# Routing stage of a mixture-of-experts trunk: one choice of experts for the last two tiles, rows of slots in a matmul pass of their own, weighing on GpSimd, five low weight parts made early

## Chip, cores and metric

One core of a Trainium2 chip runs one program. The metric is the device time of one execution in microseconds (us). TensorE (PE), VectorE (DVE), ScalarE (ACT), GpSimd (POOL) and SyncE (SP, which here issues DMAs) run their own instruction streams and meet only at semaphores.

## What is computed

A decoder layer for 2048 tokens of width 1024: token mixing (gMLP and stick-breaking attention), cross-attention to 256 memory tokens, then a mixture of experts and a last norm. The change lies between the cross-attention and the experts:

```python
g_logits = t @ w_group + b_group;  p_group = softmax(g_logits);  g_sel = argmax(g_logits)
e_logits = (t @ w_router + b_router).reshape(T, 4, 8)[:, g_sel]
top_v, top_i = top_k(e_logits, 2)
gates = p_group[g_sel] * softmax(top_v);  eid = g_sel * 8 + top_i
# tokens sorted by expert, each expert padded to blocks of 128 slots
y = (silu(xb @ w1[e]) * (xb @ w3[e])) @ w2[e]        # per block of 128 slots
out = rmsnorm(x + sum over the two choices of gate * y)
```

## The kernel before

The program is a chain of blocks; between two of them all engines meet at a barrier, so the last engine to finish one sets the start of the next. All work is in tiles of 128 tokens (16 tiles). Products in full precision are made as three products of high and low parts (`split_product`, L73): high is a rounded copy by ACT, low is DVE's difference of the raw value and the high one.

**Cross block** (`attend_memory`, the step function is written once for each engine, and `rounds` calls it with b from -2 to 16). Step b has the scores of tile b+1, the output product of tile b and, for tile b-1, the residual sum, its norm (`hm_sb`, the input of the experts) and the logits: PE turns `hm_sb` (`turn_hm`, L1637), ACT makes the high part (L1499), DVE the low one (`low_hm`, L1542), PE multiplies with the router's weights (L1720), ACT copies the 72 rows of parts out (L1514), PE adds the parts (L1732), DVE adds the bias (`add_bias`, L1576). In the last step (b = 16) only the logits of tile 15 are left. DVE also chooses the experts there (`Picks.choose`, 22 small dependent operations from L1781 to L1801): tiles 0 to 13 in the step of b = 15, tile 14 in the step of b = 16, ahead of the bias of tile 15.

**Route block** (`route`, L1902). DVE chooses tile 15, then the gates; PE counts the ranks (`rank_ps`, L2053 to L2059); DVE makes from them the slot of each of 32 pairs of a choice and a tile (to L1995). Then, in four chunks of 8 pairs with two buffers, DVE makes `equal` (L2003: which of 66 blocks), `in_slot` (L2005: which of 128 lanes) and `in_block[..., 0]` (L2008: `equal` times the token number), ACT `in_block[..., 1]` (L2045: `equal` times the gate), and PE sums 32 products `in_slot` x `in_block` of 132 columns (L2069) into `slot_ps`, which holds the row and the gate of every slot. DVE copies both out (L2011, L2012), makes the tables of the blocks' experts (L2015 to L2021); POOL gathers the 128 rows of the first block from DRAM (L1885, L1890). Beside this SP loads the first two sets of expert weights, and ACT makes the eight high parts of the first set (L1875).

**Expert block** (`run_experts`). DVE makes the eight low parts of the first set (`cut_w13`, L1879), PE transposes the gathered rows (`transpose_x(0)`, L2319), ACT and DVE cut them (L2235, L2283), and the first product into `exp_g_ps` can begin. From there PE runs through all blocks of slots; SP loads an expert's weights as soon as PE has left the buffer.

`keep_busy` (L80) is a row of products of the identity with itself, whose result nobody reads. It stands at the start of the route block (16), behind the ranks (20), and in the expert block before (20) and behind (20) the first transposes.

```python
def keep_busy(pe, out, ident, count):
    for _ in range(count):
        pe.matmul(out, ident, ident, start=True, stop=True)
```

## Time and profile before

| | |
|---|---|
| median of 3 runs | 2640.78 us (2640.08 to 2641.35) |
| the profiled execution: own time, span | 2640.34 us, 2638.6 us |
| mean granted clock of TensorE | 0.981 |
| PE busy, PE weight load, DVE, ACT, POOL (share of the span) | 95%, 78%, 57%, 49%, 23% |
| cross block ends, route block starts | 1687.9 us, 1689.3 us |
| route block ends, expert block starts | 1720.8 us, 1721.3 us |
| first product of the experts | 1732.8 us |

Times in the trace are from the start of the span. A row of the timeline has its start, its duration, the engine and line, the tile written and those read, the shape, how many instructions are merged, and in brackets how long the engine was idle before it and who released it. A full-precision product on the identity or on the slots is two rows each ("x40" for 20 products); a transpose is one.

### The profile page before, as it was taken

What the parts mean: (1) busy time and instruction counts of PE and PEld (TensorE: products, weight loads), DVE (VectorE), ACT (ScalarE), POOL (GpSimd) and SP (SyncE); (2) the same over time, 40 slices, a digit from 0 to 9 for tenths busy, and PEclk for the clock granted to TensorE, in tenths of its full rate; (3) what the DMA queues carried; (4) which work ended last, traced back from release to release, by engine and by line L of the source; (5) the groups of instructions that cost most, each with busy time, mean ns of one, the idle gap of its engine ahead of it and who ended that gap; (6) DMA issues with size and microseconds to landing.
All of it is one profiled execution on the core that took longest, in us unless ns stands there. A gap on an engine that the chain in (4) does not pass through costs nothing. (4 is left out here: it accounts for less than half of the span.)

```text
span 2638.6 us, 44762 instructions
## 1 busy us (share of the span) xinstructions
PE 2507.8 (95%) x14474; PEld 2046.1 (78%) x14475; DVE 1497.0 (57%) x1976; ACT 1291.7 (49%) x2303; POOL 604.5 (23%) x653
## 2 busy tenths in 40 slices
PE   9999999999999999999999999799999999999991
PEld 7888888676666678886888888678877888888880
DVE  5221343698888864444333433666988755565653
ACT  5221211698899941133223322346878654465643
POOL 0000011477777720000000000012212212112223
PEclk9999999999999999999999999899999999999996
DMA  7433231314201033233121221448999865586757
GB/s 268 166 122 123 84 149 43 101 34 149 73 18 45 2 120 114 98 152 106 64 88 72 90 75 67 188 139 302 391 372 375 294 205 205 196 292 209 262 163 274
DMA packets 141439, 414.83 MB, mean 157 GB/s; under 512 B 22016, under 2 KB 30720, under 8 KB 140288
## 3 DMA queue, kind: packets, MB, share of 16 engines
q1 hardware_dynamic: 125040, 371.15, 38.1%
q0 software_dynamic: 13968, 33.59, 5.4%
q10 hardware_dynamic: 2304, 8.39, 0.8%
q8 instruction: 81, 1.33, 0.2%
q14 instruction: 46, 0.38, 0.0%
HBM read 338.60 MB, written 91.75 MB: 163 GB/s over the span
## 5 line engine op out<-in xcount | busy, mean ns | idle before, releaser
L685 POOL TENSOR_TENSOR stick_weight<-stick_weight,stick_left 128x512 f32<-128x512 f32 (+3 forms) x320 | 327.8, 1038 | 126.6 <-DVE stick_left L817 122.0
L1879 DVE TENSOR_TENSOR moe_w_lo<-moe_w_lo_raw,moe_w_hi (+1 forms) x256 | 298.9, 1220 | 62.7 <-ACT moe_w_hi L1875 34.7
L1875 ACT CAST moe_w_hi<-moe_w_lo_raw (+1 forms) x256 | 256.4, 1052 | 49.7 <-DMA moe_w_lo_raw<-in_w 32.0
L817 DVE TENSOR_TENSOR_SCAN stick_left<-stick_z_ps,stick_left,stick_any_row 128x512 f32<-128x512 f32 x192 | 240.2, 1275 | 35.2 <-ACT stick_z_ps L780 34.9
L778 ACT ACTIVATE stick_weight<-stick_z_ps 128x512 f32<-128x512 f32 (+3 forms) x320 | 173.7, 543 | 32.7 <-PE stick_z_ps L727 21.2
L740 PE MATMUL stick_t_ps<-all_ident,stick_weight 128*128 128x128 f32 x1088 | 165.0, 281 | 19.0 <-DVE stick_weight_t L825 9.2
L780 ACT ACTIVATE stick_z_ps<-stick_z_ps 128x512 f32<-128x512 f32 (+3 forms) x320 | 165.7, 518 | 10.2
L740 PEld LDWEIGHTS stick_t_ps<-all_ident,stick_weight 128*128 128x128 f32 x1088 | 115.6, 141 | 70.0 <-issue 45.4
L75 PE MATMUL exp_g_ps<-moe_w_hi,exp_x_hi 128*128 x376 | 151.2, 402 | 10.8 <-DVE exp_x_lo L2283 10.8
L1890 POOL DMA_INDIRECT moe_xg<-hm_scratch,moe_now x50 | 66.6, 1331 | 403.4 <-PE exp_x_ps L2319 296.3
L75 PE MATMUL proj_z_ps<-proj_w_hi,proj_h_hi 128*128 128x512 f32 x384 | 152.1, 396 | 2.5 <-DVE proj_h_lo L403 2.5
L2307 DVE TENSOR_TENSOR moe_w_lo<-moe_w_lo_raw,moe_w_hi 128x1024 f32 (+1 forms) x128 | 148.2, 1218 | 8.6 <-ACT moe_w_hi L2269 8.2
L75 PE MATMUL exp_y_ps<-moe_w_hi,exp_h_hi 128*128 128x512 f32 x376 | 150.4, 400 | 2.3 <-DVE exp_h_lo L2303 2.3
L76 PE MATMUL proj_z_ps<-proj_w_lo,proj_h_hi 128*128 128x512 f32 x384 | 150.2, 391 | 0.0
L77 PE MATMUL proj_z_ps<-proj_w_hi,proj_h_lo 128*128 128x512 f32 x384 | 150.0, 391 | 0.0
L77 PE MATMUL exp_y_ps<-moe_w_hi,exp_h_lo 128*128 128x512 f32 x376 | 147.0, 391 | 0.0
L77 PE MATMUL exp_g_ps<-moe_w_hi,exp_x_lo 128*128 x376 | 146.8, 390 | 0.0
L76 PE MATMUL exp_y_ps<-moe_w_lo,exp_h_hi 128*128 x376 | 146.7, 390 | 0.0
L77 PE MATMUL exp_u_ps<-moe_w_hi,exp_x_lo 128*128 x376 | 146.6, 390 | 0.0
L76 PE MATMUL exp_g_ps<-moe_w_lo,exp_x_hi 128*128 x376 | 146.5, 389 | 0.0
L75 PE MATMUL exp_u_ps<-moe_w_hi,exp_x_hi 128*128 x376 | 146.3, 389 | 0.0
L76 PE MATMUL exp_u_ps<-moe_w_lo,exp_x_hi 128*128 x376 | 146.3, 389 | 0.0
(299 smaller groups left out, 5828.4 us busy)
## 6 DMA issues: line engine op xcount, KB each, us to landing
moe_w_lo_raw<-in_w SPq DMA_DIRECT2D x384, 512.0 KB
proj_w_lo_raw<-in_w_in SPq DMA_DIRECT2D x40, 256.0 KB, 6.3
proj_xs<-in_x SPq DMA_DIRECT2D x16, 512.0 KB, 4.6
qt_scratch<-proj_qk_out SPq DMA_DIRECT2D x16, 512.0 KB, 2.8
kt_scratch<-proj_qk_out SPq DMA_DIRECT2D x16, 512.0 KB, 2.7
mix_q<-qt_scratch SPq DMA_DIRECT2D x16, 512.0 KB
mix_out_xs<-in_x SPq DMA_DIRECT2D x16, 512.0 KB, 4.5
x_scratch<-mix_out_xs SPq DMA_DIRECT2D x16, 512.0 KB, 3.0
```

The source lines that it names most:

```text
L75: pe.matmul(out, left_hi, right_hi, start=first, stop=False)
L76: pe.matmul(out, left_hi, right_lo, start=False, stop=False)
L77: return pe.matmul(out, left_lo, right_hi, start=False, stop=last)
L685: nc.gpsimd.tensor_tensor(taken, taken, after, ALU.mult).then_inc(weight_done, 1)
L740: last = nc.tensor.transpose(t_ps[:, n % 2, b], weight[:, n % W_SLOTS, b * P:(b + 1) * P], ident)
L778: nc.scalar.activation(weight[:, n % W_SLOTS, 0:keys], z, ACT.Sigmoid).then_inc(take_done, 1)
L780: nc.scalar.activation(z, z, ACT.Sigmoid, scale=-1.0).then_inc(leave_done, 1)
L817: nc.vector.tensor_tensor_scan(row[:, c * BANK:c * BANK + keys][:, ::-1], back, any_row[:, 0:keys], start, ALU.mult, ALU.bypass).then_inc( ...
L1875: nc.scalar.copy(self.w13_hi[:, self.w13_at(e, i)], self.w13_raw[:, self.w13_at(e, i)]).then_inc(self.w13_cut, 1)
L1879: ops.tensor_tensor(self.w13_lo[:, self.w13_at(e, i)], self.w13_raw[:, self.w13_at(e, i)], as_f32(self.w13_hi[:, self.w13_at(e, i)]), ALU. ...
L1890: nc.gpsimd.indirect_dma_start(out=self.xg[:], out_offset=None, in_=self.hm, in_offset=bass.IndirectOffsetOnAxis(ap=self.now[:].bitcast(U3 ...
L2307: nc.vector.tensor_tensor(w2_lo[:, w2_at(e, i)], w2_raw[:, w2_at(e, i)], as_f32(w2_hi[:, i]), ALU.subtract).then_inc(w2_ready, 1)
```

## The change

1. `Picks.choose` for tile 14 is taken out of the cross block's last step; the route block chooses tiles 14 and 15 in one call.
2. In the cross block `keep_busy` is added: 10 products behind the transposes of tile 14, 8 before and 10 behind those of tile 15. In the route block 16 becomes 18, 20 stays, and 10 are added at the end; in the expert block 20 and 20 become 6 and 10.
3. The four chunks have buffers of their own (the waits on `slotted` and `gated` go). DVE makes only `equal` and `in_slot`; the product with the token number (`in_rows`) is made by POOL; ACT writes `in_gates`. PE makes 32 products of 66 columns with `in_rows` into `slot_ps`, then 32 of 66 columns with `in_gates` into `gate_ps`.
4. DVE makes one low weight part of the first set before it takes the rows of slots, four behind the tables of the blocks, and then copies the gates; the expert block makes the other three.

```diff
                     if isinstance(b, int) and b == tiles:
                         add_bias(tiles - 1)
-                        dve.wait_ge(logit_out, tiles - 1)
-                        picks.choose(nc, link, tiles - 2, 1)
...
                     if there(b, -1) and not is_last(b):
+                        if is_end(b):
+                            keep_busy(nc.tensor, z_ps[:, 0:P], ident, 8)
                         turn_hm(b)
+                        if is_end(b):
+                            keep_busy(nc.tensor, z_ps[:, 0:P], ident, 10)
...
                     if is_last(b):
                         turn_hm(b)
+                        keep_busy(nc.tensor, z_ps[:, 0:P], ident, 10)
...
-                picks.choose(nc, link, tiles - 1, 1)
+                picks.choose(nc, link, tiles - 2, 2)
...
-                    if c >= DEPTH:
-                        dve.wait_ge(slotted, (c - DEPTH + 1) * CHUNK)
-                        dve.wait_ge(gated, (c - DEPTH + 1) * CHUNK)
-                    nc.vector.tensor_tensor(equal[:, c % DEPTH], block_no[:].unsqueeze(1).broadcast_to(rows_wide),
+                    nc.vector.tensor_tensor(equal[:, c], block_no[:].unsqueeze(1).broadcast_to(rows_wide),
                                             dest_part[:, 0, k, span].unsqueeze(2).broadcast_to(rows_wide), ALU.is_equal).then_inc(marked, 1)
-                    nc.vector.tensor_tensor(in_slot[:, c % DEPTH], lanes[:].unsqueeze(1).broadcast_to(slots_wide),
+                    nc.vector.tensor_tensor(in_slot[:, c], lanes[:].unsqueeze(1).broadcast_to(slots_wide),
                                             dest_part[:, 1, k, span].unsqueeze(2).broadcast_to(slots_wide), ALU.is_equal).then_inc(marked, 1)
-                    dve.wait_ge(marked, 2 * c + 1)
-                    nc.vector.tensor_tensor(in_block[:, c % DEPTH, :, 0], equal[:, c % DEPTH], token[:, span].unsqueeze(2).broadcast_to(rows_wide),
-                                            ALU.mult).then_inc(weighed, 1)
+                for i in range(EARLY[0]):
+                    store.low_w13(nc.vector, dve, 0, i)
                 dve.wait_ge(slotted, pairs)
-                link(nc.vector.tensor_scalar(slot_rows[:], slot_ps[:, 0], float(consts.far), None, ALU.add), "slot_rows")
-                link(nc.vector.tensor_copy(slot_gates[:], slot_ps[:, 1]))
+                link(nc.vector.tensor_scalar(slot_rows[:], slot_ps[:], float(consts.far), None, ALU.add), "slot_rows")
...
+                for i in range(EARLY[0], sum(EARLY)):
+                    store.low_w13(nc.vector, dve, 0, i)
+                dve.wait_ge(spread, pairs)
+                link(nc.vector.tensor_copy(slot_gates[:], gate_ps[:]))
...
                 nc.gpsimd.memset(store.xg[:], 0.0).then_inc(store.xg_cleared, 1)
+                for c, (k, first) in enumerate(chunks):
+                    pool.wait_ge(marked, 2 * c + 1)
+                    nc.gpsimd.tensor_tensor(in_rows[:, c], equal[:, c], token[:, first:first + CHUNK].unsqueeze(2).broadcast_to([P, CHUNK, blocks]),
+                                            ALU.mult).then_inc(weighed, 1)
...
-                keep_busy(nc.tensor, slot_ps[:].rearrange("p k b -> p (k b)")[:, 0:P], ident, 16)
+                keep_busy(nc.tensor, warm_ps[:], ident, 18)
...
                 for n in range(pairs):
                     c, at = n // CHUNK, n % CHUNK
                     pe.wait_ge(marked, 2 * c + 2)
                     pe.wait_ge(weighed, c + 1)
+                    nc.tensor.matmul(slot_ps[:], in_slot[:, c, at], in_rows[:, c, at], start=n == 0, stop=n == pairs - 1).then_inc(slotted, 1)
+                for n in range(pairs):
+                    c, at = n // CHUNK, n % CHUNK
                     pe.wait_ge(gated, n + 1)
-                    nc.tensor.matmul(slot_ps[:].rearrange("p k b -> p (k b)"), in_slot[:, c % DEPTH, at],
-                                     in_block[:, c % DEPTH, at].rearrange("p k b -> p (k b)"), start=n == 0, stop=n == pairs - 1).then_inc(slotted, 1)
+                    nc.tensor.matmul(gate_ps[:], in_slot[:, c, at], in_gates[:, c, at], start=n == 0, stop=n == pairs - 1).then_inc(spread, 1)
+                keep_busy(nc.tensor, warm_ps[:], ident, 10)
...
-                cut_w13(0, range(rows))
+                cut_w13(0, range(EARLY, rows))
...
-                keep_busy(nc.tensor, g_ps[:, 0:P], ident, 20)
+                keep_busy(nc.tensor, g_ps[:, 0:P], ident, 6)
                 transpose_x(0)
-                keep_busy(nc.tensor, g_ps[:, 0:P], ident, 20)
+                keep_busy(nc.tensor, g_ps[:, 0:P], ident, 10)
```

PE's program at the end of the cross block and the start of the route block, before (`cross_s_ps` receives the turned `hm_sb`, `cross_h_ps` the logits):

```order
L1637 MATMUL cross_s_ps<-all_ident,kv_cross_work 128x128 x8
L1720 MATMUL cross_h_ps<-cross_hm_parts,cross_w_cut 72x256 x8
L1732 MATMUL cross_h_ps<-cross_both_parts,cross_parts 128x36 x2
L1637 MATMUL cross_s_ps<-all_ident,kv_cross_work 128x128 x8
L1720 MATMUL cross_h_ps<-cross_hm_parts,cross_w_cut 72x256 x8
L1732 MATMUL cross_h_ps<-cross_both_parts,cross_parts 128x36 x2
L1370 UNCONDITIONAL_BRANCH
L2048 UNCONDITIONAL_BRANCH
L82 MATMUL route_slot_ps<-all_ident 128x128 x16
```

The same place in the changed kernel:

```order
L1639 MATMUL cross_s_ps<-all_ident,kv_cross_work 128x128 x8
L82 MATMUL cross_z_ps<-all_ident 128x128 x10
L1727 MATMUL cross_h_ps<-cross_hm_parts,cross_w_cut 72x256 x8
L1739 MATMUL cross_h_ps<-cross_both_parts,cross_parts 128x36 x2
L82 MATMUL cross_z_ps<-all_ident 128x128 x8
L1639 MATMUL cross_s_ps<-all_ident,kv_cross_work 128x128 x8
L82 MATMUL cross_z_ps<-all_ident 128x128 x10
L1727 MATMUL cross_h_ps<-cross_hm_parts,cross_w_cut 72x256 x8
L1739 MATMUL cross_h_ps<-cross_both_parts,cross_parts 128x36 x2
L1374 UNCONDITIONAL_BRANCH
L2062 UNCONDITIONAL_BRANCH
L82 MATMUL route_warm_ps<-all_ident 128x128 x18
```

The identity products stand in the three places where PE had nothing to do, ahead of work that others release.

DVE's program in the route block from the last chunk's masks on, before:

```order
L2003 TENSOR_TENSOR route_equal<-pre_block_no,route_dest_part 128x528
L2005 TENSOR_TENSOR route_in_slot<-pre_lanes,route_dest_part 128x1024
L2008 TENSOR_TENSOR route_in_block<-route_equal,pre_token 128x8x66
L2011 TENSOR_SCALAR all_slot_rows<-route_slot_ps 128x66
L2012 COPY all_slot_gates<-route_slot_ps 128x66
L2015 TENSOR_SCALAR route_expert_f<-route_row_ps 1x66
L2016 CAST all_block_expert<-route_expert_f 1x66
```

The same place in the changed kernel:

```order
L2012 TENSOR_TENSOR route_equal<-pre_block_no,route_dest_part 128x528
L2014 TENSOR_TENSOR route_in_slot<-pre_lanes,route_dest_part 128x1024
L1886 TENSOR_TENSOR moe_w_lo<-moe_w_lo_raw,moe_w_hi 128x1024
L2019 TENSOR_SCALAR all_slot_rows<-route_slot_ps 128x66
L2022 TENSOR_SCALAR route_expert_f<-route_row_ps 1x66
L2023 CAST all_block_expert<-route_expert_f 1x66
...
L2028 CAST all_block_kind<-route_fresh 1x66
L1886 TENSOR_TENSOR moe_w_lo<-moe_w_lo_raw,moe_w_hi 128x1024 x4
L2032 COPY all_slot_gates<-route_gate_ps 128x66
```

The product with the token number has left DVE (it is `route_in_rows` on POOL now, four times 128x528, between the clearing of `xg` and the gather), and five low weight parts have come in.

PE's program from the ranks to the first product of the experts, before:

```order
L2062 MATMUL route_row_ps<-all_ident,route_expert_col 1x128
L82 MATMUL route_slot_ps<-all_ident 128x128 x20
L2069 MATMUL route_slot_ps<-route_in_block,route_in_slot 128x132 x32
L1942 UNCONDITIONAL_BRANCH
L2311 UNCONDITIONAL_BRANCH
L82 MATMUL exp_g_ps<-all_ident 128x128 x20
L2319 MATMUL exp_x_ps<-all_ident,moe_xg 128x128 x8
L82 MATMUL exp_g_ps<-all_ident 128x128 x20
```

The same place in the changed kernel:

```order
L2076 MATMUL route_row_ps<-all_ident,route_expert_col 1x128
L82 MATMUL route_warm_ps<-all_ident 128x128 x20
L2082 MATMUL route_slot_ps<-route_in_rows,route_in_slot 128x66 x32
L2086 MATMUL route_gate_ps<-route_in_gates,route_in_slot 128x66 x32
L82 MATMUL route_warm_ps<-all_ident 128x128 x10
L1954 UNCONDITIONAL_BRANCH
L2328 UNCONDITIONAL_BRANCH
L82 MATMUL exp_g_ps<-all_ident 128x128 x6
L2336 MATMUL exp_x_ps<-all_ident,moe_xg 128x128 x8
L82 MATMUL exp_g_ps<-all_ident 128x128 x10
```

One pass of 32 products has become two, and 10 identity products stand ahead of the barrier where there were none.

## Rows read from the trace of the kernel before

**Rows 1.** Waits of PE in the experts, 1733 to 2600 us: total, times, longest

```profile
PE exp_g_ps L75 <- DVE exp_x_lo L2283: 10.8, 11, 2.0
```

**Rows 2.** Timeline of PE, end of the cross block

```profile
1673.86 1.19 PE L1720 MATMUL cross_h_ps<-cross_hm_parts,cross_w_cut 128*72 128x256 f32 x8 [2.54 <-DVE cross_hm_parts L1542]
...
1678.69 1.97 PE L1637 MATMUL cross_s_ps<-all_ident,kv_cross_work 128*128 128x128 f32 x8 [2.12 <-DVE kv_cross_work L1597]
1683.34 1.96 PE L1720 MATMUL cross_h_ps<-cross_hm_parts,cross_w_cut 128*72 128x256 f32 x8 [2.68 <-DVE pre_logits L1576]
1685.75 1.07 PE L1732 MATMUL cross_h_ps<-cross_both_parts,cross_parts 72*128 72x36 f32 x4 [0.46 <-ACT cross_parts L1514]
```

**Rows 3.** Timeline of DVE, choices of experts and the last bias

```profile
1666.25 0.62 DVE L1797 TENSOR_REDUCE cross_pick_e_least<-cross_pick_e_work 128x14 f32<-128x448 f32 x1
...
1687.07 0.19 DVE L1797 TENSOR_REDUCE cross_pick_e_least<-cross_pick_e_work 128x1 f32<-128x32 f32 x1
...
1687.72 0.20 DVE L1576 TENSOR_TENSOR pre_logits<-cross_h_ps,cross_b_logit 128x36 f32<-128x36 f32 x1
1689.38 0.16 DVE L1781 TENSOR_REDUCE cross_pick_g_max<-pre_logits 128x1 f32<-128x4 f32 x1 [1.47 <-PEq L33]
...
1693.67 0.17 DVE L1801 TENSOR_TENSOR cross_pick_both<-cross_pick_pick 128x32 bf16<-128x32 bf16 x1
```

**Rows 4.** Timeline of PE, route block: ranks and the pass over the slots

```profile
1695.87 0.38 PE L2053 MATMUL route_rank_ps<-cross_pick_both,pre_before 128*128 128x512 bf16 x1
...
1707.75 7.33 PE L2069 MATMUL route_slot_ps<-route_in_block,route_in_slot 128*128 128x132 f32 x48 [2.21 <-ACT route_in_block L2045]
1715.88 2.04 PE L2069 MATMUL route_slot_ps<-route_in_block,route_in_slot 128*128 128x132 f32 x16 [0.81 <-DVE route_in_slot L2005]
```

**Rows 5.** Timeline of DVE and of ACT, route block: masks of the slots, gates

```profile
1705.18 0.71 DVE L2003 TENSOR_TENSOR route_equal<-pre_block_no,route_dest_part 128x528 f32<-128x528 f32 x1
1705.81 1.22 DVE L2005 TENSOR_TENSOR route_in_slot<-pre_lanes,route_dest_part 128x1024 f32<-128x1024 f32 x1
...
1714.06 2.03 ACT L2045 ACTIVATE route_in_block<-route_equal,route_gates 128x66 f32<-128x66 f32 x8 [0.83 <-DVE route_equal L2003]
```

**Rows 6.** Stretches of 1 us: busy by engine, PE's granted clock, DMA

```profile
1709.00:1710.00 1.00, 1.00 (x7) 1.00 (x6) 1.00 (x2) 1.00 (x6) 0.00 (x0) 0.50 1.04 418
```

**Rows 7.** POOL's products in the attention, grouped by shape: busy us, mean ns

```profile
L685 POOL TENSOR_TENSOR stick_weight<-stick_weight,stick_left 128x512 f32<-128x512 f32 x224 | 266.5, 1197 | 110.5 <-DVE stick_left L817 106.8 <-ACT stick_weight L778 0.7
```

**Rows 8.** Timeline of POOL and of DVE, one POOL copy at two places

```profile
2079.34 1.13 POOL L2201 COPY exp_rows_now<-all_slot_rows 128x1 int32 x1 [4.61 <-ACT exp_y L2260]
...
2097.71 0.18 POOL L2201 COPY exp_rows_now<-all_slot_rows 128x1 int32 x1 [4.99 <-ACT exp_y L2260]
...
2079.21 1.22 DVE L1879 TENSOR_TENSOR moe_w_lo<-moe_w_lo_raw,moe_w_hi  x1
```

**Rows 9.** Timeline of POOL and of DVE, end of the route block

```profile
1719.50 1.29 POOL L1890 DMA_INDIRECT moe_xg<-hm_scratch,moe_now  x1 [1.07 <-issue]
...
1719.79 0.18 DVE L2021 CAST all_block_kind<-route_fresh 1x66 int32<-1x66 f32 x1
1721.33 9.17 DVE L1879 TENSOR_TENSOR moe_w_lo<-moe_w_lo_raw,moe_w_hi 128x1024 fp32r<-128x1024 f32 x8 [1.36 <-PEq L33]
```

**Rows 10.** Timeline of PE, start of the expert block

```profile
1721.33 6.33 PE L82 MATMUL exp_g_ps<-all_ident 128*128 128x128 f32 x40 [3.41 <-PEq L33]
1727.49 1.05 PE L2319 MATMUL exp_x_ps<-all_ident,moe_xg 128*128 128x128 f32 x8
1728.38 4.63 PE L82 MATMUL exp_g_ps<-all_ident 128*128 128x128 f32 x40
1732.80 0.49 PE L75 MATMUL exp_g_ps<-moe_w_hi,exp_x_hi 128*128 x1
```

**Rows 11.** Timeline of ACT and of DVE, cuts of the first block's rows

```profile
1728.58 1.07 ACT L2235 CAST exp_x_hi<-exp_x_ps 128x512 fp32r<-128x512 f32 x2 [12.49 <-PE exp_x_ps L2319]
...
1730.42 1.28 DVE L2283 TENSOR_TENSOR exp_x_lo<-exp_x_ps,exp_x_hi 128x512 fp32r<-128x512 f32 x2
```

More of the change, by code:

```diff
@@ L1356, in is_last, with is_end @@
             return isinstance(b, int) and b == tiles - 1
+        def is_end(b):
+            return isinstance(b, int) and b == tiles
         def is_first(b):
@@ L1901, in route @@
     blocks = slot_rows.shape[1]
-    DEPTH, CHUNK = 2, 8
+    CHUNK, EARLY = 8, (1, 4)
     with ExitStack() as stack:
@@ L1924, in route @@
         spare = store.at + 4 * store.set_size
-        in_slot = s.over("in_slot", [P, DEPTH, CHUNK, P], F32, spare)
-        in_block = s.over("in_block", [P, DEPTH, CHUNK, 2, blocks], F32, spare + 4 * DEPTH * CHUNK * P)
-        equal = s.over("equal", [P, DEPTH, CHUNK, blocks], F32, spare + 4 * DEPTH * CHUNK * (P + 2 * blocks))
-        assert spare + 4 * DEPTH * CHUNK * (P + 3 * blocks) <= picks.at and picks.end <= store.at + 8 * store.set_size
+        pairs = 2 * tiles
+        chunks = [(k, first) for k in range(2) for first in range(0, tiles, CHUNK)]
+        per_pair = [P, len(chunks), CHUNK, blocks]
+        in_rows = s.over("in_rows", per_pair, F32, spare)
+        in_gates = s.over("in_gates", per_pair, F32, spare + 4 * pairs * blocks)
+        in_slot = s.over("in_slot", [P, len(chunks), CHUNK, P], F32, store.at + 8 * store.set_size)
+        equal = s.over("equal", per_pair, F32, store.lo_at + 8 * store.set_size + 4 * store.w2_size)
+        assert spare + 8 * pairs * blocks <= picks.at and picks.end <= store.at + 8 * store.set_size
+        assert pairs * P <= store.w2_size and pairs * blocks <= store.w2_size
         expert_f = s.sbuf("expert_f", [1, blocks])
@@ L1932, in route @@
         total_ps = s.psum("total_ps", [P, experts])
-        slot_ps = s.psum("slot_ps", [P, 2, blocks])
+        slot_ps = s.psum("slot_ps", [P, blocks])
+        gate_ps = s.psum("gate_ps", [P, blocks])
+        warm_ps = s.psum("warm_ps", [P, P])
         row_ps = s.psum("row_ps", [1, P])
         stepped, exped, ranked, rowed = s.sem("stepped"), s.sem("exped"), s.sem("ranked"), s.sem("rowed")
-        marked, weighed, gated, slotted = s.sem("marked"), s.sem("weighed"), s.sem("gated"), s.sem("slotted")
-        pairs = 2 * tiles
-        chunks = [(k, first) for k in range(2) for first in range(0, tiles, CHUNK)]
+        marked, weighed, gated, slotted, spread = s.sem("marked"), s.sem("weighed"), s.sem("gated"), s.sem("slotted"), s.sem("spread")
         marks = {}
@@ L2043, in _ @@
                         act.wait_ge(marked, 2 * c + 1)
-                        wait_past(act, slotted, (c - DEPTH + 1) * CHUNK)
-                    nc.scalar.activation(in_block[:, c % DEPTH, at, 1], equal[:, c % DEPTH, at], ACT.Copy,
+                    nc.scalar.activation(in_gates[:, c, at], equal[:, c, at], ACT.Copy,
                                          scale=gates[:, k, first + at:first + at + 1]).then_inc(gated, 1)
@@ L2062, in _ @@
                 nc.tensor.matmul(row_ps[:], expert_col[:], ident, start=True, stop=True).then_inc(rowed, 1)
-                keep_busy(nc.tensor, slot_ps[:].rearrange("p k b -> p (k b)")[:, 0:P], ident, 20)
+                keep_busy(nc.tensor, warm_ps[:], ident, 20)
                 for n in range(pairs):
@@ L2109, in run_experts @@
     w2_at = store.w2_at
-    LEAD = 1
+    LEAD, EARLY = 1, 5
     with ExitStack() as stack:
```

## The prediction

> **What bounds the kernel now.** I read the page first: PE is busy 95% of the span, so a change counts only where PE stands still or does work nobody needs. Then I read the waits inside the experts, then the timeline of each engine from 1670 to 1745 us. In the experts PE waits 10.8 us in 11 pieces for low parts, out of 867 us [rows 1], and SP loads a later expert's weights only when PE has left the buffer. So whatever moves the first product of the experts, at 1732.80 us [rows 10], should move the end by the same amount; that one time is what I predict. The path to it is a chain: end of the cross block, barrier, choice, ranks, masks, pass over the slots, gather, barrier, transposes, cuts. The timeline also shows PE's clock: it is at 0.50, its lower level of 1.2 GHz, in the cross block's end, where eight transposes take 1.97 us [rows 2] against 1.05 at 2.4 GHz [rows 10], and again at 1709 in the pass over the slots [rows 6], after 2.21 us without work [rows 4].
>
> **1. End of the cross block.** PE ends the last logits at 1685.75 + 1.07 = 1686.82 [rows 2], but DVE adds the bias only at 1687.72, behind the choice for tile 14 [rows 3]: taking that away gives 0.9 us. If the identity products hold the clock up, the transposes fall from 1.97 to 1.05 (0.9), the logits from 1.96 to the 1.19 that the same eight took at 1673.86 while the clock was mostly up (0.8), and the parts from 1.07 to half (0.5). The added products cost nothing here: ten take 2.3 us at the upper level (20 in 4.63 [rows 10]), and the gaps they stand in are 2.54, 2.12 and 2.68 us [rows 2]. Were the clock low, ten would take 3 us (seven rows, 3.5 products, in the 1 us of [rows 6]) and run over by 0.5. Sum: 3.1 us earlier, bounds 0.4 and 3.3.
>
> **2. Choice and ranks.** The block's choice runs from 1689.38 to 1693.84 [rows 3], but PE starts the ranks at 1695.87 [rows 4]: its 16 identity products, mostly at the lower level, end 2 us too late. Two tiles make the wide operations 64 instead of 32 elements: by 0.19 us at 32 and 0.62 at 448 [rows 3] that is 1.03 ns an element, 0.033 us for each of some 14 operations, 0.5 us in all. Choice done 4.95 us after the start; 18 products at the upper level take 4.2. Ranks start after 5.0 us instead of 6.5: 1.5 earlier, 1.0 if the clock is low. From the ranks to the masks nothing is changed, so the masks start 4.6 us earlier, at 1700.6 instead of 1705.18 [rows 5].
>
> **3. Masks and rows of slots.** Before, this took from 1705.18 to the end of the pass at 1717.92 [rows 4, 5]: 12.7 us. Now DVE needs 0.63 us (`equal`, to the next start) and 1.22 (`in_slot`) for each chunk [rows 5], 7.1 in four, and POOL multiplies beside it. POOL has no such product in this block; the nearest row is its product of two 128x512 tiles, 1.20 us [rows 7], so 1.23 for 528. The Trainium skill (GPSIMD Engine Reference, Instruction dispatch) gives some 2.5 cycles an element for two inputs; at its 1.2 GHz that is an estimate of 1.10 us, and the sum would be 0.5 us shorter.
> The question is whether the two run side by side. In the attention they do, but there DVE's scans and copies read from PSUM. Where DVE runs operations with two SBUF inputs, POOL waits: the same 128x1 copy takes 0.18 us at 2097.71 and 1.13 at 2079.34, where it ends at 2080.47 with DVE's subtraction (2079.21 + 1.22 = 2080.43) [rows 8]. Both masks have two SBUF inputs. The Trainium skill says the same (GPSIMD Engine Reference, Specifications): the interfaces are shared, with contention against DVE instructions that have two SBUF inputs. By that rule the kernel takes what I forecast, without it the first rival's time; the trace agrees with the rule.
> I take it that they **take turns**: POOL gets in when a mask ends, as the copy did, and DVE's next mask waits. A chunk is then 0.63 + 1.22 + 1.23, with the handovers 3.1 us; four are 12.4, and PE's eight products behind the last take 2.04 [rows 4]: 14.5 us, 1.8 longer than before. The bounds are 9.6 us (no waiting: PE starts after 2.1 and needs 7.5 for 32 products) and 17.2 (below). The low weight part that DVE makes behind the masks (1.15 us, eight in 9.17 [rows 9]) hides behind POOL's last product and PE. Rows of slots ready: 1715.1 us, 2.8 earlier than before.
>
> **4. Pass of the gates and barrier.** New on PE, and ahead of the barrier: 32 products. They load the same 128x128 weights as the identity products (0.232 us each) and stream fewer columns than the old ones (2.04 / 8 = 0.255): 7.4 to 8.2 us, I take 7.5. ACT has its 32 copies (2.03 us for eight [rows 5]) long done. Ten identity products add 2.3. PE ends at 1724.9. The next block began 0.54 us after POOL's end and 1.36 after DVE's [rows 9]; either may be the barrier's own time, I take 0.95: the expert block starts at 1725.9, **4.5 us later than before**. What is hidden behind PE here: the tables of the blocks, four low parts (4.6 us), the copy of the gates, and the gather, which starts 2.8 us earlier and in the old kernel was waited for by nobody, since PE was still in its 20 identity products.
>
> **5. Start of the experts.** Before: 20 products (6.33 us, partly at the lower level), transposes, 20 products (4.63), together 11.47 us. Now 6 products (1.4) and transposes (1.05); then ACT's and DVE's cuts, 1.07 + 1.28 [rows 11] with 0.1 for the handovers, against 10 products in 2.3: 2.45. Together 4.9 us. DVE's three remaining low parts take 3.45 us and end as its cut begins. The first product starts at 1730.8 instead of 1732.8.
>
> **Sum:** rows of slots 3.1 + 1.5 - 1.8 = 2.8 us earlier. From there to the expert block's start 7.5 + 2.3 + 0.95 = 10.75 us instead of the old 3.41 (1717.92 to 1721.33): 7.3 later. Start of the experts 11.47 - 4.9 = 6.6 shorter. 2.8 - 7.3 + 6.6: about 2.0 us faster. The profiled execution took 2640.34, its span 2638.6; its own time becomes 2638.3. The median shown lies 0.44 above it, so I forecast 2638.8 us. One stretch of lower clock, as at 1709 us, is likely while PE waits for POOL (2.04 of every 3.1 us busy): each costs 0.8 us, two would make 2640.3. This case's own range is 2637.8 to 2640.5; its chance is 44%.
>
> **Rivals.**
> *No waiting between POOL and DVE (22%).* The pass ends 4.9 us sooner, everything behind it too: 2633.9 us. For it speaks that the row of the copy shows a start held back, not a long product beside DVE; against it, that both masks are of the kind that held it.
> *A half-way case (13%)*: both slow down, but overlap; 2636.4.
> *POOL is starved (10%)*: it gets in only when DVE's queue of masks is empty. DVE is busy for 7.1 + 1.2 = 8.4 us, POOL's first product ends at 9.7, PE then needs 7.5: 17.2 us instead of 14.5, and the clock falls in the long wait: 2641.5 to 2642.5. Against it: the copy got in at the first boundary.
> *The clock stays down (3%)*, the case on the slower side. Identity and slot products are on the path from the ranks to the experts. At 0.3 us instead of 0.232 the gains of parts 1 and 2 shrink from 4.6 to 1.5, the last chunk and the gates' pass take 2.5 more, 26 identity products and the transposes 2.5 more: 8.1 us lost, 2647 us. It is slower than before once PE is at the lower level for more than about a quarter of that path. Against it: in the changed kernel PE has no gap over 3.1 us.
> *Given back later (5%)*: the first product is earlier but DMA bounds the experts, 2640.8. Against it: the loads are released by PE's own progress. Another 3% is for what I do not see.
>
> **How the numbers follow.** A change of 0.2%, 5.3 us, is about what a measurement of this kernel tells from none. Only the case without waiting is beyond it, with the best part of the half-way one: faster 24%. Slower needs the clock case: 3%. The rest, 73%, is within. The range reaches from the case without waiting to the near end of the starved one: 2633.3 to 2641.5 us.
>
> **What would show it.** Right: POOL's four `in_rows` end right behind DVE's `in_slot`, 3.1 us apart; DVE shows gaps or long `equal` between them; the block's rows are ready 14.5 us after the first mask; the expert block starts near 1725.9 and its first product near 1730.8; the ranks start 5.0 us into the block and PE's clock is 1.00 from 1671 to the masks. Wrong: `in_rows` of 1.2 us beside running masks (first rival), all four behind the low weight part (starved), 0.50 before the masks (clock), or a first product 2 us earlier with the same end (given back).

## Result and the profile after

The changed kernel takes 2650.49 us (median of 7 runs, 2649.53 to 2654.40), the kernel before beside it 2640.27 (2639.88 to 2641.35): a ratio of 1.004, 95% interval 1.003 to 1.0051. It is 10.2 us slower, where 2.0 us faster was forecast. The profiled span is 2649.0 us against 2638.6.

From the page of the changed kernel, its first lines, busy time by engine:

```profile
span 2649.0 us, 44928 instructions
...
PE 2528.5 (95%) x14569; PEld 2066.5 (78%) x14571; DVE 1494.5 (56%) x1951; ACT 1291.7 (49%) x2303; POOL 607.9 (23%) x657
```

PE is busy for 20.7 us more than before (2507.8), its share is still 95%, and its waits together are shorter (120.5 us of the span against 130.8): the time was not lost in waits, but inside instructions. A part of the 20.7 is wanted: the 28 identity products added in the cross block's end take 6.8 us there. Where the rest is, the timeline of PE shows, from the end of the cross block to the first products of the experts (start, duration, instruction, in brackets the idle time before it; `PEq`, PE's own sequencer, stands there at the barriers):

```profile
1670.08 1.03 PE L1639 MATMUL cross_s_ps<-all_ident,kv_cross_work 128*128 128x128 f32 x8
...
1678.46 1.09 PE L1639 MATMUL cross_s_ps<-all_ident,kv_cross_work 128*128 128x128 f32 x8 [0.69 <-DVE kv_cross_work L1601]
...
1682.24 1.14 PE L1727 MATMUL cross_h_ps<-cross_hm_parts,cross_w_cut 128*72 128x256 f32 x8 [0.45 <-DVE pre_logits L1580]
1683.83 0.64 PE L1739 MATMUL cross_h_ps<-cross_both_parts,cross_parts 72*128 72x36 f32 x4 [0.46 <-ACT cross_parts L1518]
1686.17 6.96 PE L82 MATMUL route_warm_ps<-all_ident 128*128 128x128 f32 x36 [1.70 <-PEq L33]
1693.18 1.80 PE L2069 MATMUL route_rank_ps<-cross_pick_both,pre_ones 128*128 128x480 bf16 x15
...
1705.17 1.97 PE L2082 MATMUL route_slot_ps<-route_in_rows,route_in_slot 128*128 128x66 f32 x16 [0.92 <-POOL route_in_rows L2039]
1707.80 9.69 PE L2082 MATMUL route_slot_ps<-route_in_rows,route_in_slot 128*128 128x66 f32 x48 [0.66 <-POOL route_in_rows L2039]
1717.29 13.86 PE L2086 MATMUL route_gate_ps<-route_in_gates,route_in_slot 128*128 128x66 f32 x64
1730.94 4.58 PE L82 MATMUL route_warm_ps<-all_ident 128*128 128x128 f32 x20
1736.39 1.58 PE L82 MATMUL exp_g_ps<-all_ident 128*128 128x128 f32 x12 [0.88 <-PEq L33]
1737.81 1.05 PE L2336 MATMUL exp_x_ps<-all_ident,moe_xg 128*128 128x128 f32 x8
...
1741.61 0.49 PE L75 MATMUL exp_g_ps<-moe_w_hi,exp_x_hi 128*128 x1 [0.52 <-DVE exp_x_lo L2300]
```

The cross block's end goes at the upper level now (1.09, 1.14 and 0.64 us where [rows 2] have 1.97, 1.96 and 1.07). Then one row stands out: the gates' pass. A product is two instructions here, so 64 are 32 products, and they take 13.86 us, 0.433 each, in a stretch in which PE waits for nothing. Stretches of 1 us, with PE's granted clock behind the five busy times:

```profile
1684.00:1685.00 1.00, 0.46 (x4) 0.35 (x4) 0.20 (x1) 0.00 (x0) 0.00 (x0) 1.00 0.00 0
1685.00:1686.00 1.00, 0.00 (x0) 0.00 (x0) 0.00 (x0) 0.00 (x0) 0.00 (x0) 0.50 0.00 0
...
1700.00:1701.00 1.00, 1.00 (x6) 1.00 (x6) 0.97 (x2) 0.78 (x2) 0.00 (x0) 0.50 1.03 406
...
1708.00:1709.00 1.00, 1.00 (x11) 1.00 (x10) 1.00 (x2) 0.74 (x4) 0.70 (x1) 0.95 1.02 406
1709.00:1710.00 1.00, 1.00 (x6) 1.00 (x6) 1.00 (x2) 1.00 (x6) 1.00 (x1) 0.50 1.05 418
...
1734.00:1735.00 1.00, 1.00 (x7) 1.00 (x6) 0.00 (x0) 0.00 (x0) 0.00 (x0) 0.50 0.00 0
...
1757.00:1758.00 1.00, 1.00 (x4) 0.81 (x3) 1.00 (x2) 1.00 (x3) 0.00 (x0) 0.50 0.89 352
```

The clock falls to 0.50 (1.2 GHz) just before 1709 us, in the pass over the slots, and stays there for 27 us, with PE 100% busy up to the barrier at 1735.5; before, it fell at the same place [rows 6], but was back within 4 us, in a stretch of 1 us of the kernel before:

```profile
1713.00:1714.00 1.00, 1.00 (x11) 1.00 (x10) 0.69 (x2) 0.23 (x1) 0.00 (x0) 1.00 1.04 418
```

In the changed kernel it comes back only behind the ten identity products that follow the gates' pass. There are three shorter stretches at 0.50: from 1685 to 1691.6, from 1698.8 to 1702 in the 20 identity products ahead of the slots' pass (6.36 us, before 4.73; they end at 1704.25, still before the first chunk is ready at 1705.03), and at 1757, in the second expert block. The masks, on DVE and POOL:

```profile
1702.26 0.71 DVE L2012 TENSOR_TENSOR route_equal<-pre_block_no,route_dest_part 128x528 f32<-128x528 f32 x1
1702.88 1.22 DVE L2014 TENSOR_TENSOR route_in_slot<-pre_lanes,route_dest_part 128x1024 f32<-128x1024 f32 x1
1703.05 1.98 POOL L2039 TENSOR_TENSOR route_in_rows<-route_equal,pre_token 128x528 f32<-128x528 f32 x1 [15.97 <-DVE route_equal L2012]
1704.02 1.57 DVE L2012 TENSOR_TENSOR route_equal<-pre_block_no,route_dest_part 128x528 f32<-128x528 f32 x1
...
1705.67 1.98 POOL L2039 TENSOR_TENSOR route_in_rows<-route_equal,pre_token 128x528 f32<-128x528 f32 x1 [0.65 <-DVE route_equal L2012]
```

POOL's product starts beside `in_slot` and ends at 1705.03, 0.93 us after `in_slot` has ended (1704.10); DVE's next `equal` takes 1.57 instead of 0.71 us. They take turns, 2.63 us a chunk.

From the kernel before to the changed one, in us against the rows of before: the route block starts 3.2 earlier (1686.17 against 1689.38 [rows 3]), the masks 2.9 earlier (1702.26 against 1705.18 [rows 5]), the expert block 15.1 later (1736.39 against 1721.33 [rows 10]), its first product 8.8 later (1741.61 against 1732.80), the span ends 10.4 later.

### The profile page after: what moved, and what is told of

The parts are those of the page before. It is cut to its first block and busy times, and to the rows that moved or that the text cites. A ratio compares the mean times of both kernels' runs of the same rounds, so it can differ in the third digit from the quotient of the medians.

```text
span 2649.0 us, 44928 instructions
## 1 busy us (share of the span) xinstructions
PE 2528.5 (95%) x14569; PEld 2066.5 (78%) x14571; DVE 1494.5 (56%) x1951; ACT 1291.7 (49%) x2303; POOL 607.9 (23%) x657
## 5 line engine op out<-in xcount | busy, mean ns | idle before, releaser
L780 ACT ACTIVATE stick_z_ps<-stick_z_ps 128x512 f32<-128x512 f32 (+3 forms) x320 | 165.7, 518 | 10.2
```

The source lines that it names most:

```text
L780: nc.scalar.activation(z, z, ACT.Sigmoid, scale=-1.0).then_inc(leave_done, 1)
```

## The experiments

Two theories at first. **Columns:** PE stays at the lower level through a pass of 66 columns once the clock has fallen, and not through one of 132. **Handover:** POOL makes PE wait chunk by chunk, and the waits hold the clock down.

**e1, both passes with 132 columns.** Each product streams its 66 columns twice, so that PE has more to do and computes the same.

```diff
-                    nc.tensor.matmul(slot_ps[:], in_slot[:, c, at], in_rows[:, c, at], ...
+                    nc.tensor.matmul(slot_ps[:], in_slot[:, c, at], in_rows[:, c, at].unsqueeze(1).broadcast_to([P, 2, blocks]), ...
-                    nc.tensor.matmul(gate_ps[:], in_slot[:, c, at], in_gates[:, c, at], ...
+                    nc.tensor.matmul(gate_ps[:], in_slot[:, c, at], in_gates[:, c, at].unsqueeze(1).broadcast_to([P, 2, blocks]), ...
```

> The changed kernel, but both passes stream 132 columns (the same 66 twice, the second half of the result unread), so PE does more work. Theory A (the columns that PE streams decide whether the clock comes back: the passes of 66 columns, bound by their weight loads, leave it at the lower level, those of 132 bring it back): after its fall near 1709 us the granted clock is 1.00 again within 4 us, 32 products of the gates take about 8.5 us instead of 13.9, the first product of the experts starts near 1733 instead of 1741.6, time 2640 to 2642. Theory B (PE's waits for POOL in the masks bring the clock down, and any products at the lower level keep it there): clock 0.50 through both passes, time 2650 to 2652.

Measured: 2640.34 us (median of 10) against 2640.26, ratio 0.9998 (0.9988 to 1.0007). Timeline of PE (this execution is 2.7 us late from before the cross block's end on):

```profile
1715.87 2.04 PE L2082 MATMUL route_slot_ps<-route_in_rows,route_in_slot 128*128 128x132 f32 x16 [0.58 <-POOL route_in_rows L2039]
1717.75 7.39 PE L2086 MATMUL route_gate_ps<-route_in_gates,route_in_slot 128*128 128x132 f32 x64
1724.98 2.39 PE L82 MATMUL route_warm_ps<-all_ident 128*128 128x128 f32 x20
```

and a stretch of 1 us in its slots' pass:

```profile
1709.00:1710.00 1.00, 1.00 (x10) 0.84 (x8) 1.00 (x2) 1.00 (x6) 1.00 (x1) 1.00 1.00 397
```

Twice the columns, and 10.2 us faster. PE waits for POOL just as in the changed kernel (0.58 against 0.66 us a chunk), yet the clock falls in neither pass; the expectation had it fall and come back. Between the starts of the first slot product and of the experts' first lie 25.48 us here and 36.44 there: 2.36 of the difference in the slots' pass, 6.42 in the gates' pass, 2.18 in the ten identity products and the barrier behind them. This is the loss.

**e2, the gates' pass alone with 132 columns** (the second pair of lines above).

> The changed kernel, only the pass of the gates streams 132 columns. Theory A: the clock stays at 0.50 in the pass of the slots (rows ready near 1717.5 as in the changed kernel) and comes back within 4 us of the gates' pass, which then takes 9 to 10 us instead of 13.9: time 2643 to 2646. Theory B: gates' pass 13 us or more, time 2650.

Measured: 2643.43 us in one execution. The slots' pass is the changed kernel's, clock lost at 1709, but in the gates' pass it comes back (timeline of PE, then two stretches of 1 us in that pass):

```profile
1707.81 9.69 PE L2082 MATMUL route_slot_ps<-route_in_rows,route_in_slot 128*128 128x66 f32 x48 [0.66 <-POOL route_in_rows L2039]
1717.29 9.98 PE L2086 MATMUL route_gate_ps<-route_in_gates,route_in_slot 128*128 128x132 f32 x64
```

```profile
1719.00:1720.00 1.00, 1.00 (x6) 1.00 (x6) 0.93 (x3) 0.00 (x0) 0.91 (x1) 0.50 0.00 0
1722.00:1723.00 1.00, 1.00 (x9) 1.00 (x8) 1.00 (x2) 0.00 (x0) 0.00 (x0) 0.75 0.94 381
```

**e3, DVE multiplies by the token numbers instead of POOL.**

```diff
+                    dve.wait_ge(marked, 2 * c + 1)
+                    nc.vector.tensor_tensor(in_rows[:, c], equal[:, c], token[:, span].unsqueeze(2).broadcast_to(rows_wide),
+                                            ALU.mult).then_inc(weighed, 1)
...
-                for c, (k, first) in enumerate(chunks):
-                    pool.wait_ge(marked, 2 * c + 1)
-                    nc.gpsimd.tensor_tensor(in_rows[:, c], equal[:, c], ...
```

> The changed kernel, with the product with the token number made by DVE again (POOL makes none). DVE's chunk is then 0.63 + 1.14 + 0.63 = 2.4 to 2.5 us against the 2.63 of the changed kernel. Theory A: the clock falls in the masks or soon after as before and stays down through both passes; time 2648 to 2651. Theory B (the handover between POOL and DVE is what costs): no stretched masks, clock up, time 2640 to 2643.

Measured: 2646.96 us in one execution. A chunk takes 2.37 instead of 2.63 us, so POOL's part costs 0.26 a chunk, some 1 us in all. PE's waits shrink to 0.40 us and the clock falls only at 1712, but then the gates' pass is as slow as ever. The time is 1 us under what the expectation gave for this; the stretch at 0.50 in the second expert block, worth 1.6 us, did not come in this execution (timeline of PE):

```profile
1711.75 3.52 PE L2081 MATMUL route_slot_ps<-route_in_rows,route_in_slot 128*128 128x66 f32 x16 [0.40 <-DVE route_in_rows L2017]
1715.07 13.86 PE L2085 MATMUL route_gate_ps<-route_in_gates,route_in_slot 128*128 128x66 f32 x64
```

The handover theory falls as the explanation of the 10 us.

**e5, 20 identity products between the two passes.** It asks whether 66 columns lose the clock by themselves.

```diff
+                keep_busy(nc.tensor, warm_ps[:], ident, 20)
                 for n in range(pairs):
                     c, at = n // CHUNK, n % CHUNK
                     pe.wait_ge(gated, n + 1)
```

> The changed kernel with 20 identity products between the pass of the slots and the pass of the gates. They bring PE to its upper level (behind the gates' pass they did it in 4 to 5 us), so the gates' pass starts there. If what loses the clock are the waits in the slots' pass, and 66 columns only fail to win it back, the gates' pass runs at the upper level: 7.4 to 7.6 us instead of 13.86, the 20 products 6 to 8 us, net 0 to 2 us longer: 2650 to 2652. If a pass of 66 columns loses the clock by itself, although PE never waits in it, it starts at 0.23 us a product and ends at 0.43: 10 to 12 us, 2654 to 2656.

Measured: 2647.81 us in one execution: 20 products more, and 2.7 us less than the changed kernel's median. Timeline of PE, then a stretch of 1 us in the gates' pass:

```profile
1717.83 6.17 PE L82 MATMUL route_warm_ps<-all_ident 128*128 128x128 f32 x40
1723.84 7.26 PE L2087 MATMUL route_gate_ps<-route_in_gates,route_in_slot 128*128 128x66 f32 x64
```

```profile
1725.00:1726.00 1.00, 1.00 (x11) 1.00 (x11) 0.00 (x0) 0.00 (x0) 0.00 (x0) 1.00 0.00 0
```

So the gates' pass holds the upper level when it starts at it (0.227 us a product); it doesn't win it back when it starts at the lower one. In these traces either level lasts as long as the pass does. The expectation's own sum was off by 2 to 4 us; 2.1 of them it left out: the ten products behind the pass now take 2.45 instead of 4.58 us.

**p1 and p2, the first two parts alone, on the kernel before.** p2 is the merged choice; p1 adds the identity products of the cross block's end and 18 instead of 16 at the routing's head.

```diff
-                        dve.wait_ge(logit_out, tiles - 1)
-                        picks.choose(nc, link, tiles - 2, 1)
...
-                picks.choose(nc, link, tiles - 1, 1)
+                picks.choose(nc, link, tiles - 2, 2)
```

> The kernel before with the merged choice alone, no identity product added. Both readings: the last logits' bias 0.9 us earlier, while the choice in the routing block grows by 0.5 us and stays hidden behind 16 identity products at the lower level; 0.9 us earlier in all, 2639.4, clock in the cross block's end still 0.50.

> The kernel before with the first two parts of the change alone: one choice for the last two tiles, the identity products in the cross block's end, 18 instead of 16 at the head of the routing block. Masks, pass and expert start are those of before. By the prediction: 3.1 us from the cross block and 1.5 from the choice, ranks at about 1691.3, the time 2635.7. By the reading of the changed kernel's trace (the clock falls in the barrier, so the 18 products take 7 us and cover the choice): only the 3.1 us, ranks near 1693, the time 2637.3 to 2637.6, if the rest keeps its lengths. If an earlier routing block only moves a wait, 2640.

Measured: p2 2638.62 us (ratio 0.9996, 0.9986 to 1.0006), p1 2638.31 (0.9993, 0.9983 to 1.0003), before 2640.27; neither can be told from no change. Timeline of PE in p1:

```profile
1684.46 0.63 PE L1735 MATMUL cross_h_ps<-cross_both_parts,cross_parts 72*128 72x36 f32 x4 [0.46 <-ACT cross_parts L1514]
1686.80 7.00 PE L82 MATMUL route_slot_ps<-all_ident 128*128 128x128 f32 x36 [1.70 <-PEq L33]
1693.85 1.80 PE L2058 MATMUL route_rank_ps<-cross_pick_both,pre_ones 128*128 128x480 bf16 x15
...
1728.78 0.50 PE L75 MATMUL exp_g_ps<-moe_w_hi,exp_x_hi 128*128 x1 [0.64 <-DVE exp_x_lo L2286]
```

Against its own first transposes (1670.71, before 1670.28) the route block starts 3.0 us earlier: the first part's term. The choice is done at 1691.74, the 18 products at 1693.80: the second part's 1.5 us is covered by products at the lower level, as the second reading had it. The first product is 4.0 us earlier than before, more than these parts account for, because in this execution the clock is at 1.00 through the slots' pass and the experts' start (its 20 identity products there take 4.70 us, not the 6.33 of [rows 10]); 1.6 of it is given back in the second expert block, and more in a stretch at 0.50 at 2576, in the last one (both below), so that the span, 2637.4 us, is only 1.2 shorter than before. The median of p1 is 0.7 to 1.0 us above the second reading's. p2 gained 1.65 us of medians where 0.9 was expected, inside what the runs can tell.

**e4 and g3, one pass of 132 columns over rows and gates** in the otherwise changed kernel, with POOL weighing (e4) or DVE (g3, the edit of e3).

```diff
-                    nc.tensor.matmul(slot_ps[:], in_slot[:, c, at], in_rows[:, c, at], ...
-                for n in range(pairs):
-                    c, at = n // CHUNK, n % CHUNK
                     pe.wait_ge(gated, n + 1)
-                    nc.tensor.matmul(gate_ps[:], in_slot[:, c, at], in_gates[:, c, at], ...
+                    nc.tensor.matmul(slot_ps[:].rearrange("p k b -> p (k b)"), in_slot[:, c, at],
+                                     in_block[:, c, at].rearrange("p k b -> p (k b)"), ...
```

> The changed kernel with one pass of 32 products of 132 columns for rows and gates together, as before the change; all else of the change stays (POOL weighs, five early low parts, the moved identity products). Theory A: the clock comes back within the pass, no second pass stands ahead of the barrier; rows and gates ready near 1716, the expert block waits for DVE's four low parts and starts near 1724, first product near 1729: time 2636 to 2638. If the second pass was not the trouble (theory B): clock at 0.50 from 1709 on, time 2645 or more.

> The changed kernel with one pass of 132 columns over rows and gates, and DVE multiplying by the token numbers in place of POOL. If the hand-over between DVE and POOL costs 0.26 us a chunk (2.63 against 2.37 us, as the run with DVE weighing showed), the pass ends about 1 us sooner than with POOL: 2637.2, and PE's clock stays at 1.00 through the pass. If the chunks are bound by PE (8 products of 2.04 us and their wait) instead, no difference: 2638.2.

Measured: e4 2638.16 us (0.999, 0.9981 to 1.0), g3 2636.45 (0.9988, 0.9978 to 0.9998). g3 lies 1.7 us below e4 where 1 was expected, within what the runs scatter. The split into two passes, the part that was to shorten the way to the rows of slots, is what makes the changed kernel slow: without it the kernel is 12 us faster. Against before the rest gains 2 us (e4, whose interval just reaches 1.0) to 4 us (g3, whose interval ends at 0.9998). What stands behind the pass is now the bound: DVE's four low parts hold the barrier while PE stands still, and the clock falls (timeline of PE in e4, then a stretch of 1 us at that place):

```profile
1722.64 2.90 PE L82 MATMUL exp_g_ps<-all_ident 128*128 128x128 f32 x12 [5.32 <-PEq L33]
1725.34 1.92 PE L2331 MATMUL exp_x_ps<-all_ident,moe_xg 128*128 128x128 f32 x8
```

```profile
1722.00:1723.00 1.00, 0.36 (x2) 0.39 (x3) 0.35 (x1) 0.00 (x0) 0.00 (x0) 0.50 0.00 0
```

**g4, identity products moved to where PE stands** (on g3).

```diff
-                keep_busy(nc.tensor, warm_ps[:], ident, 18)
+                keep_busy(nc.tensor, warm_ps[:], ident, 11)
...
-                keep_busy(nc.tensor, warm_ps[:], ident, 10)
+                keep_busy(nc.tensor, warm_ps[:], ident, 28)
...
-                keep_busy(nc.tensor, g_ps[:, 0:P], ident, 6)
+                keep_busy(nc.tensor, g_ps[:, 0:P], ident, 4)
```

> The kernel of the run before in this list, with the identity products moved: 11 instead of 18 at the head of the routing block (they end after the choice now, at the lower level), 28 instead of 10 behind the pass (PE stood for 5 us there and lost its clock), 4 instead of 6 at the head of the experts. If the clock is lost by idle stretches and won back by streamed columns: ranks about 1.5 us earlier, the expert block at the upper level from its start, transposes 1.05 instead of 1.9 us; 2634.5. If the 28 products only delay the barrier, or the clock falls all the same: 2637 or more.

Measured: 2634.73 us (0.998, 0.997 to 0.9989). Timeline of PE:

```profile
1686.43 5.03 PE L82 MATMUL route_warm_ps<-all_ident 128*128 128x128 f32 x22 [1.70 <-PEq L33]
...
1712.64 6.42 PE L82 MATMUL route_warm_ps<-all_ident 128*128 128x128 f32 x56
...
1721.32 1.05 PE L2330 MATMUL exp_x_ps<-all_ident,moe_xg 128*128 128x128 f32 x8
...
1725.37 0.49 PE L75 MATMUL exp_g_ps<-moe_w_hi,exp_x_hi 128*128 x1 [0.77 <-DVE exp_x_lo L2294]
```

The transposes take 1.05 us again, and the first product is 7.4 us earlier than before [rows 10]. The time is only 5.5 us lower, and the profile has the rest: two stretches at the lower level, each behind a wait for low parts. One is behind 2.0 us in the second expert block (products 0.43 us apart instead of 0.227), one behind 2.26 us in the last. The second is in the profiles of g4, p1 and e2 alone, though the wait of 2.26 us is in every run above, before and the changed kernel too (stretches of 1 us):

```profile
1741.00:1742.00 1.00, 1.00 (x4) 0.71 (x4) 1.00 (x2) 1.00 (x2) 0.00 (x0) 0.50 0.86 348
2574.00:2575.00 1.00, 1.00 (x3) 0.74 (x3) 0.00 (x0) 0.00 (x0) 0.21 (x1) 0.50 0.99 102
```

**g5 and g6, identity products in these two waits:** seven behind the first block's h transposes (g5, on g4), eight behind the last block's (g6, on g5). g5 was run a second time beside g6.

```diff
                         last.then_inc(ht_done, 1)
+                        if first:
+                            keep_busy(nc.tensor, y_ps[:, 0:P], ident, 7)
...
+                    if not more:
+                        keep_busy(nc.tensor, g_ps[:, 0:P], ident, 8)
                     if not first:
                         before = expert_of(b - 1)
```

> The retuned kernel with seven more identity products behind the first block's h transposes, where PE waits 2.0 us for the second block's low parts of x and then runs its first products at the lower level (0.43 us apart instead of 0.227). If that wait is what loses the clock, the stretch is gone and everything behind it 1.5 us earlier: 2633.2. If the time is set elsewhere by then (weights that arrive), or the stretch comes whatever PE does in the wait: 2634.7.

> The kernel of the last run with eight more identity products behind the last block's h transposes, where PE waits 2.26 us for the low parts of h; in some profiled executions (not in all) PE's clock is at 0.50 for 4 us right behind that wait, which costs 1.7 us. If that stretch is a part of the scatter between executions, the median falls by up to 0.9 us, to 2633.3, and the range of 2632.7 to 2637.0 narrows from above. If the scatter comes from elsewhere: 2634.2 and the same range.

> The kernel before in this list without those eight products, on the same chip, for the comparison: 2634.2.

Measured: g5 2634.19 us (0.9979, 0.997 to 0.9988) and again 2634.42 (2632.10 to 2636.78); g6 2633.52 (2632.50 to 2635.08) against 2639.18 for the kernel before beside it: 0.9976, 0.9967 to 0.9985. In g5 the stretch at 1741 is gone (timeline of PE, then the stretch of 1 us):

```profile
1738.03 1.73 PE L82 MATMUL exp_y_ps<-all_ident 128*128 128x128 f32 x14
1740.19 0.49 PE L75 MATMUL exp_g_ps<-moe_w_hi,exp_x_hi 128*128 x1 [0.43 <-DVE exp_x_lo L2294]
```

```profile
1741.00:1742.00 1.00, 1.00 (x6) 0.82 (x5) 1.00 (x2) 1.00 (x3) 0.00 (x0) 1.00 0.87 352
```

In the profiled executions the third block's transposes come 1.4 us earlier than in g4 (1751.22 against 1752.64), near the 1.5 expected, but of the medians only 0.5 is left, and 0.3 when each is taken against the kernel before beside it, less than they scatter. g6's median is 0.9 us below g5's on the same chip and its range 2.6 instead of 4.7 us wide, what the expectation gave for a stretch that comes in some executions. That this is the reason is not shown: none of the three profiled executions of g5 and g6 has the stretch, and with 11 runs of each the difference is within the scatter. g6 has the lowest ratio of this study, though it can't be told from g5's: 5.7 us below before, where the changed kernel is 10.2 above it.

## Why the prediction was wrong, step by step

1. **Cross block's end: right.** Forecast 3.1 us; the route block starts 3.2 us earlier, 3.0 against the kernel's own first transposes (1670.08, before 1670.28). The transposes (1.09 us) and logits (1.14) lasted about what their rows at the upper level said, the parts 0.64 where half of 1.07 was taken.
2. **Choice and ranks: wrong, 1.5 us forecast, none came.** The step that failed is "18 products at the upper level take 4.2". The clock was at 1.00 in the last parts (1684 us) and at 0.50 from 1685 on, within the 1.70 us in which PE stood at the barrier, where the change puts no identity product, and the 18 took 6.96. How long the clock stays down there differs between executions: in e4, e5 and g3 the same 18 took 5.6 to 5.7 us, so 1 us of the 1.5 would have come. The sign that was named, 1.00 from 1671 us to the masks, failed twice, here and at 1700. The choice itself was done at 1691.10, 4.93 us after its start, as forecast. The guard in the text ("1.0 if the clock is low") rested on a misread row: "seven rows, 3.5 products, in the 1 us of [rows 6]". The count of a stretch includes rows that reach in from outside it; a product at the lower level is 0.43 us, not 0.3.
3. **Masks and rows of slots: mechanism right, size off, and a term missing.** POOL and DVE take turns; by the trace above the rule that the prediction took from the Trainium skill (GPSIMD Engine Reference, Specifications) holds here. The chunk takes 2.63 us, not 3.1: POOL's product alone needs 0.93 us, not 1.23, and DVE's next mask queues without a loss. POOL's fourth product ends 10.65 us after the first mask, not 12.4, which saved 1.75 us; from there PE needed 4.6 us to the end of the pass, not 2.04, since most of its last 24 products ran at the lower level. From first mask to the rows 15.3 us (1702.26 to 1717.53), forecast 14.5.
4. **Gates' pass: this is the step that failed.** "7.4 to 8.2 us, I take 7.5" priced the products by rows at the upper level alone; it took 13.65 us to the next start, and the ten behind it 4.58 instead of 2.3. At the upper level the pass takes 7.26 (e5): the price was right, the level wrong. The bounds should have held a pass at the lower level, which [rows 6] show in the very pass that was to be split. A fall of the clock there was foreseen, but as a stretch that ends by itself and costs 0.8 us; in passes of 66 columns it did not end for 27 us.
5. **Start of the experts: right.** 5.22 us (1736.39 to 1741.61), forecast 4.9.

Put together: e1's difference of 10.96 us between first slot product and first expert product is the clock's. Taken off the changed kernel's 1741.61 it leaves 1730.65, and the forecast was 1730.8: that is luck in part, since the 1.7 us lost in part 2 and the 1.75 saved in part 3's chunks cancelled. To the 8.8 us at the first product the stretch at 1757 adds 1.6: the third blocks' transposes are 10.4 us later (1768.89 against 1758.49), and so is the end. Once the first product had moved, nothing else in the experts took or gave time, as the text had said.

The rival that came nearest to what happened was "the clock stays down", with 3%. What was held against it, "PE has no gap over 3.1 us", was true and no argument: the clock fell with PE idle for 0.66 us of every chunk. Its price, 8.1 us at 0.3 us a product, was too low for the same misread row. The range, 2633.3 to 2641.5, left this rival out. And the step from "PE has work" to "the clock is up" was never weighed against a row. The Trainium skill (TensorE: Matmul & The Clock Gate, What's actually happening) says that a monitor sets the clock by how busy PE has been lately; no run here speaks against a monitor, but by the busy time that the profile shows PE was at 100% for 27 us at 0.50, and being busy did not bring the clock back.

## What to carry to other kernels

Price every TensorE term at both clock levels, and ask of each stretch which level it enters with and what in it would win the upper one back: narrow products may keep a level and not regain it. Before splitting one product of 132 columns into two of 66 under the same weights, count that PE takes as long for half the columns, and put the wide work, or identity products, ahead of the narrow. When a kernel is 95% busy and slower, compare durations of the same instruction, not waits.

## What the runs showed of the hardware that I had not expected

- Products with 128x128 weights and 66 columns ran at either level for as long as the gates' pass lasted: 0.433 us each at 0.50 (changed kernel, e3), 0.227 at 1.00 (e5). With 132 columns, the same weights and the same start at 0.50, the clock was back after some 5 us (e2). What in the two passes makes the difference is not separated further; the load of weights shows as 100% busy in both.
- At the upper level twice the columns cost next to nothing: 7.39 us for 64 instructions of 132 columns (e1), 7.26 for 64 of 66 (e5).
- In the pass over the slots small waits lost the clock with 66 columns (0.66 us a chunk in the changed kernel, e2 and e5, 0.40 in e3) and not with 132 (0.58 in e1 and e4, 0.33 in g3, p1 and p2).
- A wait of 2.0 us in the second expert block is followed by a stretch at 0.50 in the changed kernel, e1, e4, e5, p1 and g4, and not in before, e2, e3, p2 and g3, though the wait is the same in all. It costs 1.6 us. The wait of 2.2 us ahead of the slots' pass is alike: the clock falls behind it in before and holds in g4 and g5. What decides it, no run shows. With seven identity products in the second block's wait none of three executions (g5 twice, g6) has the stretch.
